# Unscaled first value products, and a relaid seam between layer norm, pooling and output projection, in a hybrid decoder step

## The reference, cut to what matters

```python
h = rmsnorm(x, g_mix)
p = h @ w_in                       # 2048 x 3072
v, gate, u = p[..., :1024], p[..., 1024:2048], p[..., 2048:]
a = v * sigmoid(gate)
yc = silu(layernorm(depthwise_conv31(concat(state_conv, a)) + b_dw, ln_g, ln_b))
mean_w = trailing mean of u over w = 2, 4, 8, 16 positions (256 channels each)
yp = per_group((mean_w - u) @ w_pool) * pool_scale
x = x + concat([yc, yp]) @ w_out   # 2048 x 2048
x = x + hier_moe(rmsnorm(x, g_ffn))  # 32 experts, top 1 group of 4, top 2 inside
y = rmsnorm(x, g_final)            # and the new conv and pool states
```

## Time and profile before

| | us |
|---|---|
| median of 3 runs (lowest, highest) | 1355.9 (1355.44, 1358.77) |
| the profiled execution | 1355.8 |
| its span, first to last instruction | 1353.9 |
| TensorE busy | 1251.8 |
| VectorE / ScalarE / GpSimd busy | 341.9 / 121.1 / 111.0 |
| granted TensorE clock, mean | 0.98 |

### The profile page before, as it was taken

The page is one execution under the profiler, slowest core; times in us unless marked ns, Lnnn a source line. Parts: engine busy times, 40 slices in busy tenths (PEclk is TensorE's granted clock), DMA queues, the critical chain, the costliest instruction groups (busy, mean ns, idle before and its releaser), DMA issues.

```text
span 1353.9 us, 15810 instructions
## 1 busy us (share of the span) xinstructions
PE 1251.8 (92%) x6348; PEld 696.2 (51%) x6348; DVE 341.9 (25%) x690; ACT 121.1 (9%) x241; POOL 111.0 (8%) x167
## 2 busy tenths in 40 slices
PE   8999998999999998989889898998989989898894
PEld 7777776777855444434434444444344444344331
DVE  5499963010332110110101011020101111020216
ACT  2100014000410000000000000000000000000003
POOL 3211164000000100000000000000000000000000
PEclk9999999999999999999999999999999999899997
DMA  8544325664659999999999999999999999999985
GB/s 247 167 153 154 127 93 172 214 248 160 243 231 389 429 427 427 426 430 427 427 426 426 428 426 429 425 426 424 425 429 425 416 427 425 418 410 428 388 357 193
DMA packets 82887, 465.15 MB, mean 344 GB/s; under 512 B 7999, under 2 KB 50111, under 8 KB 56691
## 3 DMA queue, kind: packets, MB, share of 16 engines
q1 hardware_dynamic: 77184, 456.41, 82.6%
q0 software_dynamic: 5392, 7.87, 1.9%
q10 hardware_dynamic: 283, 0.48, 0.1%
HBM read 457.20 MB, written 20.80 MB: 353 GB/s over the span
## 4 chain that ended last, share of the span: by engine, by line
DMA 43%; PE 39%; issue 6%; DVE 4%; POOL 3%; SPq 1%; ACT 1%; DVEq 0%; POOLq 0%
DMA arena<-in_w_up_dram 40%; PE bank L777 21%; PE bank L595 11%; DVE arena L1089 3%; PE bank L755 3%; PE bank L798 3%; DMA stage<-in_w_down_dram 2%; POOL arena L1480 1%; DMA arena<-expert_rows 1%; SPq L424 1%; DMA arena<-in_g_final_dram 1%; POOL arena L1489 0%; ACT x1r L962 0%; POOL arena L1486 0%; PE bank L675 0%
## 5 line engine op out<-in xcount | busy, mean ns | idle before, releaser
L777 PE MATMUL bank<-arena,stage 128*64 128x512 f32 x1920 | 440.7, 613 | 55.7 <-DMA arena<-in_w_up_dram 55.7
L777 PEld LDWEIGHTS bank<-arena,stage 128*64 128x64 f32 x1920 | 146.1, 141 | 344.1 <-issue 306.0
L595 PE MATMUL bank<-arena,stage 128*128 128x288 f32 x1280 | 313.8, 407 | 2.9 <-ACT arena L939 1.5
L595 PEld LDWEIGHTS bank<-arena,stage 128*128 128x128 f32 x1280 | 242.7, 190 | 72.6 <-issue 4.1
L755 PEld LDWEIGHTS bank<-x1w,x1r 128*128 128x128 f32 x1536 | 173.9, 192 | 25.1 <-issue 25.1
L755 PE MATMUL bank<-x1w,x1r 128*128 128x128 f32 x1536 | 179.9, 277 | 0.0
L1335 DVE TENSOR_TENSOR a_sb<-sl_sb,bank 128x256 f32<-128x256 f32 x32 | 19.5, 610 | 494.2 <-ACT sl_sb L989 494.2
L798 PE MATMUL bank<-arena,aT 128*64 128x512 f32 x512 | 113.4, 595 | 8.5 <-ACT aT L991 8.5
L1089 DVE SCALAR_TENSOR_TENSOR arena<-arena,wdw 128x256 f32<-128x256 f32 x240 | 102.9, 504 | 0.0
L1497 POOL DMA_INDIRECT expert_rows<-ysb,cur_d x31 | 30.3, 978 | 855.5 <-DVE ysb L1355 828.9
L1355 DVE TENSOR_SCALAR ysb<-bank,wslot 128x512 f32<-128x512 f32 x31 | 23.3, 751 | 254.7 <-PE bank L798 254.7
(11 more groups left out here) (271 smaller groups left out, 461.4 us busy)
## 6 DMA issues: line engine op xcount, KB each, us to landing
arena<-in_w_gate_dram SPq DMA_DIRECT2D x48, 2048.0 KB, 14.2
arena<-in_w_up_dram SPq DMA_DIRECT2D x48, 2048.0 KB, 20.8
arena<-in_w_down_dram SPq DMA_DIRECT2D x30, 2048.0 KB, 17.6
xT<-in_w_down_dram SPq DMA_DIRECT2D x15, 2048.0 KB, 20.4
stage<-in_w_down_dram SPq DMA_DIRECT2D x15, 2048.0 KB, 21.7
arena<-in_w_gate_dram SPq DMA_DIRECT2D x16, 1536.0 KB, 15.0
arena<-in_w_up_dram SPq DMA_DIRECT2D x16, 1536.0 KB, 21.2
stage<-in_w_in_dram SPq DMA_DIRECT2D x11, 2048.0 KB, 8.3
```

The costliest lines, as they stand in the source:

```text
L595: last = pe.matmul(ps[bank][:, 0:NTOK], wsl[a][:, k, cc * P:(cc + 1) * P], rhs[:, k, :], start=(n == 0), stop=(n == KT - 1))
L777: mm = pe.matmul(ps[4 + s][BLK * h:BLK * (h + 1), :], xgT[:, k, BLK * s:BLK * (s + 1)], w[:, :, 256 * h:256 * (h + 1)], start=(k == 0), st ...
```

## The change

What it does, by place:

- Opening: the warm-ups after the first seven go. The vector of gains is turned before the last input tile. VectorE sums the squares of the first two landed tiles, then makes `xg` = x * g (no factor), then the last square sum. The first two value blocks multiply `xg`; the spreading of the factors stands in the middle of the second; ScalarE copies it from bank 4 to `rbc`. hT = xg * rbc is made after that, for the gates and all later blocks; VectorE scales the two value blocks as it evacuates them. The two fills of `x1r` move behind.
- GpSimd: `prod` lies in `ysb`, its loop is written out, and the wait after the last group is gone.
- TensorE: the first channel sum stands in the middle of block 6 of the pool inputs, the second between blocks 7 and 8. Of the first two projection blocks the convolution half comes before the last two pooled tiles.
- ScalarE: the first mean, the squares and the tables come earlier among the copies of pool inputs; swishes alternate with the copies of pooled tiles.
- Ranks: row transposes 10 and 11 stand between the two rank products in place of four warm-ups; the rows' copies write runs of 32 and read with a stride of 16.

```diff
-AWAKE_START = (7, 4, 2)
-AWAKE_SCALE = 8
+AWAKE_START = (7, 0, 0)
...
-AWAKE_ROUTE = (4, 2)
+AWAKE_ROUTE = 2
...
+        xg = [words(arena, o, CT * NTOK).rearrange("p (k t) -> p k t", k=CT) for o in (O_MIX, O_YC)]
+        rbc = words(lns, 0, NTOK)
...
-        prod = words(arena, O_ST, 2 * NS * W).rearrange("p (c t w) -> p c t w", c=2, t=NS)
+        prod = ysb[:, :, :].rearrange("p s f -> p (s f)")[:, 0:2 * NS * W].rearrange("p (c t w) -> p c t w", c=2, t=NS)
...
+                if i == TT - 1:
+                    pe.wait_ge(pv_in, 16 * 6)
+                    pe.transpose(ps[7][:, 0:64], pv[:, :], ident[0:64, 0:64]).then_inc(pvT_mm, 1)
...
-            stay_awake(AWAKE_SCALE, 6)
-            pe.wait_ge(diag_ready, 1)
-            for t in range(TT):
-                last = pe.matmul(ps[4][:, T0[t]:T0[t] + TS[t]], ones[0:TS[t], :], diag[0:TS[t], t, 0:TS[t]], start=True, stop=True)
-            last.then_inc(rbc_mm, 1)
+            def scale_rows():
+                pe.wait_ge(diag_ready, 1)
+                for t in range(TT):
...
+                last.then_inc(rbc_mm, 1)
...
+            def values_unscaled(cc, between):
+                for k in range(KT):
+                    if cc == 0:
+                        pe.wait_ge(xg_ready, k + 1)
+                        if k == KT // 2:
+                            pe.wait_ge(slot_in[0], 16)
+                    if between and k == KT // 2:
+                        between()
+                    last = pe.matmul(ps[cc][:, 0:NTOK], wsl[0][:, k, cc * P:(cc + 1) * P], xg[k // CT][:, k % CT, :],
+                                     start=(k == 0), stop=(k == KT - 1))
+                return last
...
+                pe.wait_ge(rbc_ready, 1)
...
-                dense(cc, 0, cc, hT, late=(slot_in[0], 16) if cc == 0 else None, each=hT_ready if cc == 0 else None).then_inc(vg_mm, 1)
+                values_unscaled(cc, scale_rows if cc else None).then_inc(vg_mm, 1)
...
-                dense(2 + cc, 1, cc, hT).then_inc(vg_mm, 1)
+                dense(2 + cc, 1, cc, hT, each=hT_ready if cc == 0 else None).then_inc(vg_mm, 1)
...
-                    dense(2 * c + cc, c, cc, hT).then_inc(u_mm, 1)
...
-            pe.wait_ge(sum_ready, 1)
-            channel_sum(4, sqw[:, 4:6, :]).then_inc(sum_mm, 1)
-            pool_inputs(3)
-            pe.wait_ge(sq_ready, 1)
-            channel_sum(5, sqw[:, 0:2, :]).then_inc(sumsq_mm, 1)
+                    if m == 3 and cc == 1:
+                        pe.wait_ge(sq_ready, 1)
+                        channel_sum(5, sqw[:, 0:2, :]).then_inc(sumsq_mm, 1)
+                    dense(2 * c + cc, c, cc, hT, between=sum_of_channels if m == 2 and cc == 1 else None).then_inc(u_mm, 1)
+
+            def sum_of_channels():
+                pe.wait_ge(sum_ready, 1)
+                channel_sum(4, sqw[:, 4:6, :]).then_inc(sum_mm, 1)
+
+            for m in range(4):
+                pool_inputs(m)
...
-            for i in range(CT):
...
+            def out_half(cc, h):
+                for k in range(CT * h, CT * h + CT):
+                    if h == 0 and cc == 0:
+                        pe.wait_ge(mix_ready, k + 1)
+                    last = pe.matmul(ps[cc][:, 0:NTOK], wsl[1][:, k, cc * P:(cc + 1) * P], mixT[:, k, :],
+                                     start=(k == 0), stop=(k == KT - 1))
+                return last
+
+            for i in range(6):
+                pooled(i)
+            pe.wait_ge(slot_in[1], 16 * 7)
+            out_half(0, 0)
+            pooled(6)
+            pooled(7)
+            out_half(1, 0)
             pe.wait_ge(wp_ready, CT)
-            pooled_first = tuple(range(CT, KT)) + tuple(range(CT))
+            for cc in range(2):
+                out_half(cc, 1).then_inc(o_mm, 1)
...
-            for i in range(3, 4 * TT):
+            for i in range(3, 10):
...
-                    stay_awake(AWAKE_ROUTE[0], 5)
+                    token_rows(10)
+                    token_rows(11)
...
+                if i == TT - 1:
+                    act.wait_ge(pvT_mm, 1)
+                    act.copy(pvT[:, :], ps[7][:, 0:64]).then_inc(pvT_ready, 1)
...
+            act.wait_ge(rbc_mm, 1)
+            act.copy(rbc, ps[4][:, 0:NTOK]).then_inc(rbc_ready, 1)
...
-            values(0)
...
+            for n in range(5):
                 pool_line(n)
             act.wait_ge(sum_mm, 1)
             act.activation(nmean[:, :], ps[4][:, 0:NTOK], ACT.Copy, scale=-1.0 / DC).then_inc(nmean_ready, 1)
             act.wait_ge(centred, 1)
             act.activation(words(arena, O_AW, CT * NTOK), words(arena, O_YC, CT * NTOK), ACT.Square).then_inc(squared, 1)
+            pool_line(5)
+            act.activation(preload[:, :], ones[:, 0:1], ACT.Sqrt)
             pool_line(6)
-            pool_line(7)
             act.wait_ge(var_ready, 1)
             act.activation(lnr[:, :], lnv[:, :], ACT.Sqrt).then_inc(sqrt_done, 1)
+            act.activation(silu_table[:, :], ones[:, 0:1], ACT.Silu)
+            pool_line(7)
+            act.wait_ge(yn_ready, 1)
+            for j in range(4):
+                swish(j)
             for i in range(CT):
-                act.wait_ge(wp_mm, i + 1)
-                j = CT - 2 - 2 * (i // 2) + i % 2
-                act.activation(mixT[:, CT + j, :], ps[4 + i % 2][:, 0:NTOK], ACT.Copy, scale=pps[:, j:j + 1]).then_inc(wp_ready, 1)
-            act.activation(silu_table[:, :], ones[:, 0:1], ACT.Silu)
-            act.wait_ge(yn_ready, 1)
-            for j in range(CT):
-                act.activation(mixT[:, j, :], yc[:, j, :], ACT.Silu, bias=plb[:, j:j + 1], scale=plg[:, j:j + 1]).then_inc(mix_ready, 1)
+                pooled(i)
+                if i < 4:
+                    swish(4 + i)
 
...
-                act.copy(x1p[0:TS[t], t, 32 * o:32 * o + 32, :],
-                         ps[ROWB[i % len(ROWB)]][0:TS[t], :].rearrange("r (p k) -> r p k", k=KT)).then_inc(row_evac, 1)
+                act.copy(x1r[0:TS[t], t, :].rearrange("r (k p) -> r k p", k=KT)[:, :, 32 * o:32 * o + 32],
+                         ps[ROWB[i % len(ROWB)]][0:TS[t], :].rearrange("r (p k) -> r k p", k=KT)).then_inc(row_evac, 1)
...
-            for a, b in ((NS, 2 * NS), (2 * NS, P)):
-                dve.memset(x1r[a:b, 2, :], 0.0).then_inc(rest_zero, 1)
             link(dve.memset(ss[:, :], 0.0))
...
+            for t in LANDING[:-1]:
+                square_sum(t)
+            dve.wait_ge(pvT_ready, 1)
+            for k in range(KT):
+                if k % 4 == 0:
+                    dve.wait_ge(xT_ready, 4 * (TT - 1) + k // 4 + 1)
+                dve.tensor_scalar(xg[k // CT][:, k % CT, :], xTk[:, k, :], pgm[:, k:k + 1], None, ALU.mult).then_inc(xg_ready, 1)
+            square_sum(LANDING[-1])
             dve.tensor_scalar(va[:, :], ss[:, :], 1.0 / D, EPS, ALU.mult, ALU.add).then_inc(act_in, 1)
 
...
+            dve.wait_ge(rbc_ready, 1)
+            dve.wait_ge(xg_ready, KT)
             for k in range(KT):
-                if k % 4 == 0:
...
-                dve.scalar_tensor_tensor(out=hT[:, k, :], in0=xTk[:, k, :], scalar=pgm[:, k:k + 1], in1=ps[4][:, 0:NTOK],
...
+                dve.tensor_tensor(hT[:, k, :], xg[k // CT][:, k % CT, :], rbc, ALU.mult).then_inc(hT_ready, 1)
+            for cc in range(2):
+                dve.wait_ge(vg_mm, cc + 1)
+                dve.tensor_tensor(vw[:, cc, :], ps[cc][:, 0:NTOK], rbc, ALU.mult).then_inc(v_evac, 1)
+            for a, b in ((NS, 2 * NS), (2 * NS, P)):
+                dve.memset(x1r[a:b, 2, :], 0.0).then_inc(rest_zero, 1)
...
+                    dve.wait_ge(v_evac, 2 * g + cc + 1)
...
-            with pool.Fori(0, 4) as g:
-                ch.loop(g, 1)
+            for g in range(4):
+                if g:
+                    pool.wait_ge(conv_chain, PERC * g)
...
-                pool.wait_ge(conv_chain, PERC * (g + 1))
-            ch.end(4)
+            pool.wait_ge(work_ready, 4)
```

More of the change, by code:

```diff
@@ L658, in _, with pooled @@
             pe.wait_ge(var_ready, 1)
-            for i in range(CT):
+            def pooled(i):
                 g, dd = NG - 1 - i // 2, i % 2
@@ L705, in _ @@
                 if n == 0:
-                    dense(0, a, 0, mixT, order=pooled_first, late=(mix_ready, CT)).then_inc(o_mm, 1)
                     pe.wait_ge(st_ready, 4)
@@ L742, in _ @@
             last.then_inc(rank_mm, 1)
[L743 removed]
+            stay_awake(AWAKE_ROUTE, 7)
             pe.wait_ge(row_evac, 4 * TT)
@@ L880, in _ @@
             act.activation(sq[:, :], va[:, :], ACT.Sqrt).then_inc(sqrt_done, 1)
-            act.wait_ge(pvT_mm, 1)
-            act.copy(pvT[:, :], ps[7][:, 0:64]).then_inc(pvT_ready, 1)
+            act.wait_ge(rbc_mm, 1)
+            act.copy(rbc, ps[4][:, 0:NTOK]).then_inc(rbc_ready, 1)
             def values(g):
@@ L920, in pool_line, with pooled, swish @@
                          ps[c][:, SEQ:NTOK].rearrange("p (s t) -> p s t", s=NSEQ)).then_inc(u_evac[c // 2], 1)
-            for n in range(6):
+            def pooled(i):
```

(6 more changed lines are left out.)

19 lines of the change are left out of this document (6 added, 13 removed).

## The result

Over ten runs each the kernel after takes 1351.4 us (median, 1346.2 to 1354.5), the kernel before 1358.4 (1355.4 to 1359.9): ratio 0.9945, 95% interval 0.9933 to 0.9956, about 7.5 us less (7.0 between the two medians). The prediction was 1360.0. Its direction was wrong. (The three runs of before that I started from had a median of 1355.9, 2.5 us under that of the ten.)

The account below looks back on a forecast made before the run. The prediction took the experts' weight waits as bounding most of the span, projections second, earlier gains shifting the whole stream. -3.3 - 6.7 + 13.1 (TensorE's wait) + 1.65 - 0.5 = +4.25 gave 1360.0 us, range 1349 to 1367.

Parts of the forecast that it names:

- The step that failed: Last group's taps: GpSimd's earlier pooling gets in between them, so VectorE loses the length of GpSimd's work there.
- 16.1 forecast: Last group's taps: VectorE's loss to GpSimd's pooling, 16.6 us times 0.97, bounds 0 and 16.6.
- The 97%: Taps beside GpSimd's products: VectorE loses 4.14 of GpSimd's 4.26 us, the share applied to the pooling.
- The clock term: Behind TensorE's wait at the channel sum: a lower granted clock adds 1.65 us, bounds 0 and 3.3.
- Rival A: Last group: the convolution isn't slowed, so TensorE doesn't wait at the channel sum; 1345.3 us, faster; chance 0.15.
- Opening, -3.3: Opening: unscaled value products start at 12.3 instead of 16.23; -3.3 us in sum, from -3.9 to -1.5.
- The removed warm-ups stood mostly in waits: Opening: removing TensorE's warm-up matmuls gives nothing more beyond the -3.9 us of the earlier start.
- States, +0.1: Opening: TensorE comes to the states at 29.1, the pool state lands at 29.2; +0.1 us.
- rival B: Opening: GpSimd's issue of the states waits for VectorE's new multiplications; +2.0 us, 1362.0; chance 0.06.
- Seam, -6.7: Pool inputs to projection: GpSimd's last pass, table load and swishes no longer stand between TensorE's products; -6.7 us.
- Ranks, -0.5: Ranks: fewer warm-up matmuls, row transposes in their place, changed row copies; -0.5 us, bounds -0.8 and +1.5.
- Rival C: Ranks: row copies get slower by strided reading of banks; +2.0 us against -0.5, 1362.0; chance 0.06.

Follow-up runs that it names:

- e4: The kernel after with one added wait, at the 31st of the last group's 62 taps, for the tap just before it: 1361.3 us, ratio 1.0018.
- e2: The kernel after with GpSimd's wait for the last group's taps put back ahead of the pooling: 1350.8 us, ratio 0.9940.
- e9: The kernel after with the last group's taps written out behind the loop, no wait added, as a control: 1351.4 us, ratio 0.9956.
- e10: The kernel after, last group's taps written out, with one 8-column memset between its 30th and 31st taps, no wait: 1364.1 us, ratio 1.0053.
- e11: The kernel after, last group's taps written out, with one added wait at the 57th of 62 taps: 1359.2 us, ratio 1.0016.
- e3: The kernel after with every tap of VectorE's last group waiting for the tap just before it: 1368.5 us, ratio 1.0067.
- e1: The kernel after with the six removed warm-up matmuls of the opening put back: 1351.2 us, ratio 0.9946 to before.
- e8: The kernel after with the opening's warm-ups back and the projection's last-block one-column square-sum products in three pieces: 1350.4 us, ratio 0.9934 to before.
- e7: The kernel before with the ranks' part of the change alone: 1358.0 us, ratio 0.9995.
- e6: The kernel before with the opening's part of the change alone: 1356.8 us, ratio 0.9988.
- e5: The kernel before with the seam's part of the change alone: 1352.8 us, ratio 0.9960.

## Why the prediction was wrong, step by step

**The step that failed:** "And GpSimd gets in between taps; it isn't starved." The exclusion was right and the winner wrong. I read a price from the earlier trace rows and took it for a law. Those products started at the head of a group, before VectorE's stream of overlapping taps was running; after shows such a head too, where the two first taps take 2.64 us. There GpSimd's product has its plain 2.1 us and VectorE's instruction beside it is stretched (2.29 instead of 0.42), so I read it that GpSimd was in first; the two records start within 0.02 us and don't say it by themselves, and no run puts one and the same instruction both at the head and in the middle. As e4 shows, once GpSimd is in it keeps its turns. In after the pooling asks in the middle of a closed stream, and e2 to e4, e9 and e10 show that it then gets nothing until the stream breaks. The earlier trace rows were additions of an open kind: each waits for its predecessor or for another engine. So VectorE lost 1.3 us on the taps (16.1 forecast), TensorE waited none (13.1), and there was no clock to pay for (1.65). These two terms are 14.75 us too much; the other terms below take back 5.6 of them, and 1360.0 less 9.1 is the 1350.9 of the profile.

**Two sizes in the same step.** The 97% was read too high. The gaps of 2.05 and 2.09 hold 0.24 to 0.26 us that the chain has ahead of its other taps too; the records themselves (2.30 and 2.34 us, elsewhere 0.43 and 0.47) give 3.7 of 4.26. In e4, where GpSimd does get in, the 60 taps take 40.51 us against 25.73 in before; less 1.9 for a second tap stretched at the head, two passes cost VectorE 12.9 us, not 16.1, since a tap goes through with each instruction of GpSimd. The clock term was right wherever the wait came about: 1.7 (e11), 2.0 (e4) and 2.5 us (e3, e10) from the sum to the end of the seventh block, forecast 1.65 with bounds of 0 and 3.3.

Rival A had this in a half-sentence ("GpSimd gets the port only in VectorE's pauses") at 0.15. Its time, 1345.3, was 5.6 us too low, by the terms that it shared with the forecast, and the loss from which it decides is 11.9 us by them and not 11.5. What I could have asked of rows 5: who was there first? Both that and the taps' spacing (51 start within 19.7 us in before, 155.9 to 175.6, with a median record of 475 ns, so they overlap) are in the trace of before.

The Trainium skill ("SBUF — State Buffer", Who interferes with whom) says that issue order decides who blocks, and that the first to issue has the pair for its whole instruction. I used it for the size and passed over the order. By that order the addition, which was asked for ahead of the next tap, would have had its turn behind the tap that it met; e4 agrees with that, one instruction each, but in after the hold lasts over some 40 instructions (18.9 us), which the rule doesn't tell. It also says that a VectorE instruction with at most one SBUF input, outside the two-port modes, doesn't contend with GpSimd; e10's memset letting GpSimd in agrees.

**Opening, -3.3.** The profiled pair shows -1.24 at the gates (33.81 against 35.05). "The removed warm-ups stood mostly in waits" held for neither side: TensorE ran its transposes at the lower rate to about 13 in after, while the profile of before was one of the executions with an early rise. Like with like, early with early: first value product 12.40 (e1) or 12.17 (e8) against 16.23, close to the forecast's -3.9; gates 32.41 and 32.16 against 35.05, -2.6 to -2.9. Late with late: 33.0 to 33.8 (e2, after) against 36.97 (e7), -3.2 to -4. So the mechanism was right at the gates; its size moves with the execution, and I read one execution as if it were fixed. At the end less arrives: the timed e6 gives -1.6 with an interval of -2.7 to -0.4, which leaves out my -3.3. Why is not shown, beyond the seam of e6's one profile.

**States, +0.1 (and rival B).** B's mechanism is real: GpSimd's first DMA issue (line 1491) takes 2.19 us instead of 0.76, from 15.64 to 17.83, and VectorE's multiplications (line 1107) run to 17.72. In e1, e2, e6 and e8, where these end at 16.44, 17.27, 16.84 and 16.21, the issue ends at 16.55, 17.39, 16.95 and 16.33: each 0.11 or 0.12 later. Its price was small, since TensorE comes late enough: no wait in after, 0.2 us for the pool state in e1, 0.7 in e6. The Trainium skill's rule on starved descriptors ("SBUF — State Buffer", SBUF: two separate sides) names a copy in a two-port mode; these multiplications behave in the same way.

**Seam, -6.7.** Measured -5.0 in the pair of profiles (6.24 less the opening's 1.24), e5 -5.6 in time. Mechanism right; the term was mis-sized by the sums, which I put at 0.5 each and which take 1.14 and 0.98 (the 1.13 stood in the earlier trace rows), and by the stretch behind w_out's landing, 17.8 instead of 17.2. The landing itself took 8.2, forecast 8.1.

**Ranks, -0.5.** -0.33 (6.57 at the select less 6.24). The feared strided reads of PSUM cost nothing: 578 ns a copy, where the strided writes of before took about 1.08 us (their records overlap, which is why eleven stood in 9.88). Rival C is out, and so is its bound.

**Sum.** 1355.8 - 1.24 - 5.0 - 0.33 = 1349.2 against 1350.9 in the profiled execution. The remaining 1.7 us lie in the experts, whose loads end 56.9 us of waits (55.7 before) with the same code. From the first product of the row selection to the end after took 986.7 us and before 985.1; over the profiles of all thirteen kernels, which have the same code there, it is 985.0 to 991.6, so the difference is within that spread.

## What to carry to other kernels

When VectorE and GpSimd shut each other out, ask who is in first and whether its stream ever opens, before pricing the overlap. A closed stream (taps that overlap, no other instruction between) held GpSimd for 18.9 us here and cost VectorE 1.3; one wait or one stray memset in it turned that round and cost 10 us or more. With instructions like these, work that must not hurt such a stream should be asked for in its middle, not at its head, and nothing should be slipped in between.

## What the runs showed that I had not expected

- The memory of the state: a wait or a 0.07 us memset at the middle of 62 taps costs 10 to 13 us (1361.3, 1364.1 against 1351.4), a wait near the end 8. Some 2 us of each are the lower clock behind TensorE's wait.
- TensorE's rise to full rate in the opening moves by some 5 us between the profiles of kernels with nearly the same opening, and the granted clock column shows 1.00 throughout; only the records' lengths (1.16 or 2.08 us for eight warm-ups) tell.
- A drop of the clock behind 2.2 us of one-column products at 344 us, in e1 and e2 and not in after, costs 1.7 us, more than the 1.4 us by which e1's profile had been ahead of that of after at the gates.
- ScalarE's copy of 128x512 out of a bank with stride in the read and runs in the write takes 0.58 us, half of the other way round.
